# Scores of the last attention in three reduced-precision products on row halves, and later turns of its second kind of heads

## The reference

```python
q_w = apply_rope(rms_norm(heads(wq, 8), wq_norm), cos, sin)
k_w = apply_rope(rms_norm(heads(wk, 2), wk_norm), cos, sin)
y_w = windowed_gqa(q_w, k_w, v_w, kc_w, vc_w, sink)
q_n = rms_norm(heads(nq, 8), nq_norm)
k_n = rms_norm(heads(nk_, 8), nk_norm)
y_n = neighbourhood_attention(q_n, k_n, v_n, kc_n, vc_n, rpb)
y = jnp.concatenate([y_w * jax.nn.silu(wg), y_n * jax.nn.silu(ng)], axis=-1)
```

## Time and profile before

| what | us |
|---|---|
| median of 3 runs | 1634.72 (1629.84 to 7097.55) |
| profiled execution | 1633.1 |
| its span, first to last instruction | 1631.3 |
| the 20 us from 1500: TensorE, VectorE, ScalarE busy | 17.99, 14.00, 11.72 |

### The profile page before, as it was taken

The page is one execution under the profiler, slowest core; times in us unless marked ns, Lnnn a source line. Parts: engine busy times, 40 slices in busy tenths (PEclk is TensorE's granted clock), DMA queues, the critical chain, the costliest instruction groups (busy, mean ns, idle before and its releaser), DMA issues.

```text
span 1631.3 us, 21300 instructions
## 1 busy us (share of the span) xinstructions
PE 1543.8 (95%) x8160; PEld 1236.0 (76%) x8160; DVE 972.4 (60%) x1757; ACT 778.4 (48%) x1321; POOL 63.4 (4%) x129
## 2 busy tenths in 40 slices
PE   6999999999999999999999999899968999999997
PEld 5887777799887888777899887778753477876675
DVE  4454457666445454457666556855786755685664
ACT  4546775455344446775455443345440013335652
POOL 4040000000000000000000000000000000400000
PEclk9999999999999999999999999999987999999999
DMA  8783335696555752434796553522220001542100
GB/s 252 241 181 101 111 106 198 191 274 182 198 186 191 250 180 79 129 104 155 228 258 188 191 177 125 140 78 57 73 78 13 0 27 52 137 146 62 52 1 26
DMA packets 183012, 220.94 MB, mean 135 GB/s; under 512 B 6507, under 2 KB 103317, under 8 KB 182848
## 3 DMA queue, kind: packets, MB, share of 16 engines
q1 hardware_dynamic: 179840, 211.65, 41.6%
q0 software_dynamic: 3072, 7.93, 2.5%
HBM read 216.55 MB, written 3.01 MB: 135 GB/s over the span
## 4 chain that ended last, share of the span: by engine, by line
PE 73%; DVE 16%; ACT 7%; issue 3%; DMA 1%; SPq 0%; ACTq 0%; DVEq 0%
PE bank L582 20%; PE bank L584 19%; PE bank L583 19%; DVE w_low L1650 2%; DVE arena L2027 2%; ACT w_high L1278 2%; PE bank L803 1%; PE bank L1013 1%; PE bank L1031 1%; PE bank L663 1%; PE bank L747 1%; PE bank L778 1%; PE bank L599 1%; PE bank L1136 1%; PE bank L1002 1%
## 5 line engine op out<-in xcount | busy, mean ns | idle before, releaser
L1650 DVE TENSOR_TENSOR w_low<-raw,w_high 128x1024 fp32r<-128x1024 f32 x352 | 425.2, 1214 | 405.8 <-ACT w_high L1278 400.2
L1278 ACT ACTIVATE w_high<-raw 128x1024 fp32r<-128x1024 f32 x352 | 366.7, 1046 | 369.3 <-PE bank L584 308.2
L582 PE MATMUL bank<-w_high,acts_r 128*128 128x512 f32 (+1 forms) x848 | 341.5, 403 | 20.8 <-DVE acts_r L1667 6.5
L584 PE MATMUL bank<-w_high,acts_r 128*128 128x512 f32 (+1 forms) x848 | 332.6, 392 | 0.0
L583 PE MATMUL bank<-w_low,acts_r 128*128 128x512 f32 (+1 forms) x848 | 331.8, 391 | 0.0
L582 PE MATMUL bank<-acts_r,w_high 128*128 128x256 f32 (+1 forms) x736 | 233.0, 317 | 2.2 <-DVE arena L2045 1.3
L584 PE MATMUL bank<-acts_r,w_low 128*128 128x256 f32 (+1 forms) x736 | 227.3, 309 | 0.0
L583 PE MATMUL bank<-acts_r,w_high 128*128 128x256 f32 (+1 forms) x736 | 227.0, 308 | 0.0
L582 PEld LDWEIGHTS bank<-w_high,acts_r 128*128 128x128 f32 x848 | 161.8, 191 | 63.3 <-DVE w_low L1650 12.9
L584 PEld LDWEIGHTS bank<-w_high,acts_r 128*128 128x128 f32 x848 | 160.8, 190 | 36.9
L583 PEld LDWEIGHTS bank<-w_low,acts_r 128*128 128x128 f32 x848 | 161.5, 190 | 32.6
(11 more groups left out here) (298 smaller groups left out, 1790.5 us busy)
## 6 DMA issues: line engine op xcount, KB each, us to landing
raw<-in_w_in SPq DMA_DIRECT2D x70, 1024.0 KB, 5.2
raw<-in_w_up SPq DMA_DIRECT2D x64, 512.0 KB, 6.8
raw<-in_w_down SPq DMA_DIRECT2D x32, 1024.0 KB, 5.0
raw<-in_w_ada SPq DMA_DIRECT2D x24, 1024.0 KB, 7.5
raw<-in_w_in SPq DMA_DIRECT2D x32, 512.0 KB, 4.6
raw<-in_w_o SPq DMA_DIRECT2D x8, 1024.0 KB, 7.4
raw<-in_w_out SPq DMA_DIRECT2D x8, 1024.0 KB, 5.1
raw<-in_w_out_c SPq DMA_DIRECT2D x4, 768.0 KB, 5.3
```

Of the source, the lines that this page charges most:

```text
L582: mm(o, lh, rh, start=start, stop=False)
L584: return mm(o, ll, rh, start=False, stop=stop)
L1278: run(A_(high, src, ACT.Copy), (high_ready, n + 1))
L1650: run(V.tensor_tensor(low, src, high.bitcast(F32), ALU.subtract), (split_ready, n + 1))
```

## The change

The order of units becomes: head pairs, both heads of a pair next to each other per tile. Scores of W and N are computed in pairs by the form of kind G; the odd unit of a pair issues none. For this every turned head of the layer gets a high half (ScalarE, `take_head_high`) and a low half (VectorE, `take_head_low`), in new places of the arena. The N heads are no longer turned ahead of the attention: six groups (two of queries, four of keys) are turned after units 0, 1, 5, 7, 9 and 11, each by four transposes, a ScalarE copy and a VectorE subtraction at the end of that round. The window heads keep their places on TensorE; their low halves are made on VectorE after the norms of slab 0 and slab 2.

```diff
-    return [(k, h, t) for k in ("W", "N") for h in range(QH) for t in range(TILES)]
+    return [(k, 2 * p + side, t) for k in ("W", "N") for p in range(QH // 2) for t in range(TILES) for side in range(2)]
...
+        late_heads = {0: (2, 0), 1: (2, 1), 5: (3, 0), 7: (3, 1), 9: (3, 2), 11: (3, 3)}
...
-            def turn_heads(l, j, src, chunks, tiles, per_bank):
+            def turn_heads(l, j, src, chunks, tiles, per_bank, only=None):
                 pe.wait_ge(*heads_ready.at(l, j))
-                for b in range(chunks // per_bank):
+                for b in range(chunks // per_bank) if only is None else (only,):
                     o = open_bank("heads", l, j, b)
...
                     for n, (qp, kp) in enumerate(((0, 0), (1, 0), (0, 1))):
                         for side in range(2):
                             rows = slice(DH * side, DH * (side + 1))
...
+                            if kind == "G":
+                                q, k = qT2[:, qp], kT2[:, kp, h // 4]
+                            elif kind == "W":
+                                q, k = wqT[qp], wkT[kp][:, h // 4]
+                            else:
+                                q, k = nqT[qp], nkT[kp][:, h // 2]
+                            ins = mm(o[side][:, 0:N4 - first], q[rows, h // 2, t * P:(t + 1) * P], k[rows, first:N4],
                                      start=n == 0, stop=n == 2)
...
-                    o = open_bank("s", 2 + l, u, among=ATTENTION_BANKS)
-                    ins = mm(o[:, 0:N4 - first], q[half:half + DH, h // 2, t * P:(t + 1) * P], k, start=True, stop=True)
-                    close_bank(ins, "s", 2 + l, u)
...
                     advance(filler, per_unit(u) if u < len(U) else 1000)
+                    if l == 1 and u in late_heads:
+                        turn_late_heads(*late_heads[u])
                     if u >= 2:
                         values(u - 2)
...
-            turn_heads(1, 3, lambda c, t: nk[:, t, c * P:(c + 1) * P], 4, T4, 1)
...
-            turn_heads(1, 2, lambda c, t: nq[:, t, c * P:(c + 1) * P], 4, TILES, 2)
...
+            def take_head_high(j, b, due=True):
...
+                act.wait_ge(*filled(*key))
+                x = (wqT, wkT, nqT, nkT)[j][0]
+                if j % 2:
+                    take_high(A_(x[:, b, :], bank(*key)[:, :], ACT.Copy), *key)
...
+                    if l == 1 and u in late_heads:
+                        take_head_high(*late_heads[u], due=False)
...
+            def take_head_low(j, b):
...
+                dve.wait_ge(*high_done[key])
+                high, low = (wqT, wkT, nqT, nkT)[j]
+                if j % 2:
+                    run(V.tensor_tensor(low[:, b, :], bank(*key)[:, :], high[:, b, :].bitcast(F32), ALU.subtract), emptied(*key))
...
+                    if l == 1 and u in late_heads:
+                        take_head_low(*late_heads[u])
...
             heads_norm(1, 0, wq, TILES, QH, 2, True, None, [("in2", 1, 0, t) for t in range(TILES)], after_wq)
+            for b in range(KVH):
+                take_head_low(1, b)
             heads_norm(1, 2, nq, TILES, QH, 4, False, None, [("in2", 1, 2, t) for t in range(TILES)], after_nq[0:2])
+            for b in range(2):
+                take_head_low(0, b)
```

More of the change, by code:

```diff
@@ L370, in two_blocks @@
         nv = carve(at, T4, GW)
[L371 to L376, removed]
+        in_acts = lambda n, *shape: carve([n], *shape, of=acts_r, start=base)
+        in_hidden = lambda n, *shape: carve([n], *shape, of=hidden_r, start=qkv_at)
+        assert at[0] == 19 * D and nk_at == 15 * D
+        wqT = in_hidden(19 * D, QH // 2, SEQ), in_hidden(14 * D, QH // 2, SEQ)
+        wkT = in_acts(base + 6144, KVH, N4), in_acts(base + 7168, KVH, N4)
+        nkT = in_acts(base + 4096, QH // 2, N4), in_hidden(20 * D, QH // 2, N4)
+        nqT = in_hidden(22 * D, QH // 2, SEQ), in_hidden(23 * D, QH // 2, SEQ)
+        at[0] = 24 * D
+        wgT = carve([wq_at + 1024], 4, SEQ)
         ngT = carve([nk_at + 1024], 4, SEQ)
@@ L384, in two_blocks @@
         o3_tok = carve([wq_at], TILES, GW)
-        y3_tok = carve([wq_at + 1024], TILES, GW)
+        y3_tok = carve([nk_at], TILES, GW)
         oT3 = carve([base + 4096], 4, SEQ)
@@ L964, in turn_heads, with turn_late_heads, scores @@
                     close_bank(ins, "heads", l, j, b)
+            def turn_late_heads(j, b):
+                if j == 2:
+                    turn_heads(1, 2, lambda c, t: nq[:, t, c * P:(c + 1) * P], 4, TILES, 2, b)
+                else:
+                    turn_heads(1, 3, lambda c, t: nk[:, t, c * P:(c + 1) * P], 4, T4, 1, b)
             def attention2(l, filler, per_unit):
                 U = units_of_block2(l)
-                def score_pair(u):
+                def scores(u):
                     kind, h, t = U[u]
[L972 to L975, removed]
+                    if u % 2:
+                        return
+                    first = SEQ if kind == "G" and t >= TILES else 0
+                    if kind == "G":
+                        if t == 0:
+                            pe.wait_ge(*emptied("heads", 0, 1, h // 4))
+                            pe.wait_ge(*emptied("heads", 0, 0, h // 2))
+                    elif u == 0 or U[u - 1][0] != kind:
+                        for j, n in {"W": ((0, 2), (1, 2)), "N": ((2, 2), (3, 4))}[kind]:
+                            for b in range(n):
+                                pe.wait_ge(*emptied("heads", 1, j, b))
                     o = [open_bank("s", 2 + l, u + side, among=ATTENTION_BANKS) for side in range(2)]
@@ L979, in score_pair @@
                             rows = slice(DH * side, DH * (side + 1))
-                            ins = mm(o[side][:, 0:N4 - first], qT2[rows, qp, h // 2, t * P:(t + 1) * P], kT2[rows, kp, h // 4, first:N4],
+                            if kind == "G":
+                                q, k = qT2[:, qp], kT2[:, kp, h // 4]
+                            elif kind == "W":
+                                q, k = wqT[qp], wkT[kp][:, h // 4]
+                            else:
+                                q, k = nqT[qp], nkT[kp][:, h // 2]
+                            ins = mm(o[side][:, 0:N4 - first], q[rows, h // 2, t * P:(t + 1) * P], k[rows, first:N4],
                                      start=n == 0, stop=n == 2)
@@ L1494, in take_features @@
                     run(A_(dst[c // 4][:, c % 4, :], bank(*key)[:, 0:n], ACT.Exp, scale=-1.0), silu_exp.by(l, c))
+            def take_head_high(j, b, due=True):
+                key = ("heads", 1, j, b)
+                if due:
+                    splits.due(*key)
+                act.wait_ge(*filled(*key))
+                x = (wqT, wkT, nqT, nkT)[j][0]
+                if j % 2:
+                    take_high(A_(x[:, b, :], bank(*key)[:, :], ACT.Copy), *key)
+                else:
+                    take_high(A_(x[:, 2 * b:2 * b + 2, :], bank(*key)[:, :].rearrange("p (a n) -> p a n", a=2), ACT.Copy), *key)
             def attention2(l):
@@ L1592, in _ @@
             heads_rsqrt(1, 0, TILES * QH)
-            for b in range(4):
-                copy_out(nkT[:, b, :], bank("heads", 1, 3, b)[:, :], "heads", 1, 3, b)
             for t in range(TILES):
@@ L1598, in _ @@
             for b in range(KVH):
-                copy_out(wkT[:, b, :], bank("heads", 1, 1, b)[:, :], "heads", 1, 1, b)
+                take_head_high(1, b)
             heads_rsqrt(1, 2, TILES * QH)
             for b in range(2):
-                copy_out(wqT[:, 2 * b:2 * b + 2, :], bank("heads", 1, 0, b)[:, :].rearrange("p (a n) -> p a n", a=2), "heads", 1, 0, b)
+                take_head_high(0, b)
             for t in range(T4):
                 copy_out(nv[:, t, :], bank("in2", 1, 4, t)[:, :], "in2", 1, 4, t)
-            for b in range(2):
-                copy_out(nqT[:, 2 * b:2 * b + 2, :], bank("heads", 1, 2, b)[:, :].rearrange("p (a n) -> p a n", a=2), "heads", 1, 2, b)
             attention2(1)
@@ L2046, in take_features @@
                                                in1=u[:, s, 0:SEQ - 1], op0=ALU.mult, op1=ALU.add), emptied(*key) if s else None)
+            def take_head_low(j, b):
+                key = ("heads", 1, j, b)
+                dve.wait_ge(*high_done[key])
+                high, low = (wqT, wkT, nqT, nkT)[j]
+                if j % 2:
+                    run(V.tensor_tensor(low[:, b, :], bank(*key)[:, :], high[:, b, :].bitcast(F32), ALU.subtract), emptied(*key))
+                else:
+                    k = slice(2 * b, 2 * b + 2)
+                    run(V.tensor_tensor(low[:, k, :], bank(*key)[:, :].rearrange("p (a n) -> p a n", a=2), high[:, k, :].bitcast(F32),
+                                        ALU.subtract), emptied(*key))
             def attention2(l):
```

## The result

The changed kernel takes 1640.6 us (median of five, 1640.2 to 1641.4), the kernel before 1631.4 beside it: ratio 1.0054, 95% interval 1.0037 to 1.0070. So it is slower by half a per cent: small, but told apart from none by the interval. The range held it (1624 to 1646). The medians differ by 9.2 us. The profiled executions have spans of 1638.7 and 1631.3 us: +7.4, where the sum of the prediction said +3.2. One execution of the kernel before took 7097.6 us; no run shows why, and the medians don't hang on it.

A forecast was written before the change was run, and what follows sets the result against it. The prediction took the last attention to be bound by its order of events, no engine being full and TensorE setting one step of four. Terms -2.9 - 4.4 - 2.7 + 5.7 + 3.9 + 0.8 + 2.8 = +3.2 on 1633.1 gave 1636.3 us, range 1624 to 1646.

The forecast's parts named there:

- one step of four: Last attention, groups of four units: only the 3.28 us step is set by TensorE and can profit from cheaper scores.
- Scores, first half: Last attention, three groups after unit 3: the 3.28 us step falls to a plain round of 2.3, gaining 2.9 us.
- Scores, second half: Last attention, N units: the 3.27 us step falls to 2.16 in four groups, gaining 4.4 us.
- Start: Start of the last attention, to E(3), the end of unit 3's exponent: 2.7 us gained, 1.7 of removed turns included.
- Late turns: Units 5, 7, 9, 11: VectorE's subtraction ahead of the next maximum adds 1.4 us each, +5.7 us.
- Bank 6: Units 8 and 12: TensorE's filler waits for the SiLU group's bank, +1.96 us twice, +3.9 us.
- Unit 13's late pair: Unit 13: TensorE, late with a pair of scores ahead, makes the 2.28 us step 3.04, +0.8 us.
- Clock: Behind the waits at units 8 and 12: half clock costs about 1.4 us a place, +2.8 us.
- rival C: Last attention: half clock as a habit, from 1.6 us gaps twice per group; 1657, or 1647 for every second group; chance 0.15.
- A: Whole kernel: TensorE savings pay out in full, 19 us of scores and 1.7 of turns, 1612 us; chance 0.05.
- B: Last attention: turns hide and banks don't clash, so only gains stand, 1624 to 1628, say 1625 us; chance 0.20.
- low chance that I gave to a real gain: Whole kernel: a time below 1602 us, about 2% under the kernel before, given 0.01.

The follow-up runs named there:

- after: The changed kernel itself, with nothing further edited: 1640.6 us, ratio 1.0054 to the kernel before.
- e1: Changed kernel with the six late turns allowed only the attention's banks 0 to 4: 1629.7 us, ratio 0.9980 to the kernel before.
- e5: Changed kernel with 49 dummy transposes added in a bank of their own at units 8 and 12: 1633.5 us, ratio 1.0007 to the kernel before.
- e12: e4 with 13 dummy transposes ahead of the transposes of units 4, 8 and 12, in the bank those open anyway: 1628.2 us, ratio 0.9976.
- e2: Changed kernel with the low half of each late turn made after the next unit's maximum instead of before it: 1634.0 us, ratio 1.0005.
- e4: Changed kernel with score pairs for the window heads alone; N heads turned and scored as in the kernel before, no late turns: 1630.6 us, ratio 0.9989.
- e6: Changed kernel with all six late turns moved to the end of the projections, ahead of the attention: 1630.4 us, ratio 0.9992.
- e10: Changed kernel with subtractions after the next maximum, late turns in bank 6 (unit 1's in an attention bank), SiLU groups in 5 and 7: 1623.1 us, ratio 0.9959.
- e3: Changed kernel with the edits of both e1 and e2: 1626.2 us, ratio 0.9959 to the kernel before.
- e9: e4 with 13 dummy transposes in a bank of their own ahead of the transposes of units 4, 8 and 12: 1628.9 us, ratio 0.9986.

## Why the prediction was right, and which terms were off

The sign and the shape were right: the saving of the scores falls on one step of four, two side effects of the late turns cost more than it, and the whole moves by less than 1%. The number alone would say little: gains of 10.0 and losses of 13.2 us nearly cancel in the sum, and 1640.6 is 4.3 above the 1636.3 that I wrote. What bears the prediction out is the steps. Term by term, against the profiles of after, e1 and e5:

- *Scores, first half*, forecast -2.9. Steps 7, 11 and 15 at full clock are 2.28, so 3 x 0.98 = -2.9. e12 has it alone.
- *Scores, second half*, forecast -4.4. Groups of 12.19 against 13.32, measured -4.6 with the last one.
- *Start*, forecast -2.7. E(3) came 2.9 earlier, although TensorE took up the projections 0.86 us later than before, ahead of any instruction that the change touches (1434.07, 1433.21), which lies within the scatter of the profiles (1431.90 to 1434.34). Net of that -3.8. The step that failed: I let half clock stay, and it didn't come. E(0) by itself, net -1.7, is as forecast.
- *Late turns*, forecast 4 x 1.4 (written +5.7). e1 has steps 8 and 12 at 5.88 (+1.3) and 6 at 3.52 (+1.24): about +5.1. e2 shows the order as the cause.
- *Bank 6*, forecast 2 x 1.96. e5 gives 2 x 1.8 at full clock, e1 shows the cause. The rotation followed was right for units 8 and 12.
- *Unit 13's late pair*, forecast +0.8: step 14 is 3.12 in e5, +0.84.
- *Step 10*, not in the forecast: 4.09 in e5 against 3.52 for the same turn in e1 at unit 6, so +0.6: TensorE is still late there from the clash.
- *Clock*, forecast +2.8, "about 1.4 a place". This term was mis-sized. It has 4.92 - 3.52 = 1.40 of step 6 and 0.47 of step 7, 7.40 - 5.56 = 1.84 each of 9 and 13, 5.34 - 4.09 = 1.25 of 10 and 4.15 - 3.12 = 1.03 of 14: 7.8 us. Two things were missed. The values take 1.60 at half clock, not 0.93, and lie on the chain there. And an episode that I hadn't foreseen comes at unit 5 (1500 to 1506), behind the 1.6 us gap that the cheaper scores open, which I had listed under rival C alone.

From +3.2 to +7.4 there are 4.2 us: clock +5.0, upstream +0.9, step 10 +0.6, start -1.1, turns and banks -0.9, second half -0.2, together 4.3.

Of the rivals: A fell. TensorE lost 15.3 us of work and nothing on the path came of it beyond single steps. B fell by e1 and e2, which show both mechanisms that it denied. C as a habit of all groups fell (the second half of the attention has clock 1.00), but its mechanism holds in the first half, in two of three groups of e4 and e6. I should have given it a price in the sum and not only a place among the rivals. The low chance that I gave to a real gain was right for this version; e10 shows that the idea is worth some 5 to 9 us once the late turns get places of their own.

Left open: why a wait of 1.6 us is followed by half clock in some groups and not in others, and why 2.76 us at the start of the changed kernel is not. The wait of 1.62 us at unit 4 alone has half clock behind it in the profiles of after, e2, e3, e4, e5 and e6, and none in those of e1 and e10. The mean clock over a whole execution differs too from one execution of a kernel to the next (e4: 0.975 to 0.980), so a single profile says what an episode costs, not how often it comes. That also limits the term of the clock: its 1.9 us at unit 5 are one execution's, and only the rest is tied to the clash by e5.

## What to carry to other kernels

When a helper gives out buffers by age, an added user shifts everybody's place: follow the rotation to the next owner of each, and keep a late, slow-to-empty user out of the ring of those it would block. Put a new operation on an engine behind, not ahead of, the one that the others wait for, even where the engine is a third idle. And where work is taken from a TensorE that isn't the bound, ask what fills the freed time: price the gap at half clock for all its products, and fill it only in a buffer that it holds anyway.

## What was not expected of the hardware

Adding 98 transposes (2 x 49) that compute nothing made the kernel 7.1 us faster (e5), and 39 gave 2.4 us (e12 against e4, by the medians, with intervals that just overlap), the granted clock of the stretches behind them going from 0.50 to 1.00. At half clock the values (eight rows of 64 columns, fp32) take 1.60 us instead of 0.93, and a pair of score sets 1.58 instead of 0.91 (e4: 1502.01 to 1503.59). Waits of 1.62 us (e4) brought the clock down and those of 1.62 (e10) and 2.76 (after) didn't, so the length of the last wait doesn't decide it alone. The Trainium skill, "TensorE: Matmul & The Clock Gate", Part 1, says that the gate goes by how busy the array has been of late. The runs agree as far as they go: filling the waits kept 1.00 in e5, e9 and e12, and one wait of the same size went either way.
